# Decay products by doubling on VectorE between projection halves, context units in the down-projection, radix-2 spectra, and a split last projection

## The reference, cut to what matters

```python
def second_block(...):
    h = modulate_2(rmsnorm(x, norm1_g), sh1, sc1)
    hc = modulate_2(rmsnorm(ctx, norm1_g), sh1c, sc1c)
    p, pc = h @ w_in, hc @ w_in                      # 1024 -> 3*512 (Hyena) + 5*512 (HGRN)
    y_hy = hyena_mixer(p[..., :1536], ...)           # y = x2*(h2 * (x1*(h1 * v))), long convolutions by FFT
    y_hg = hgrn_mixer(p[..., 1536:], pc[..., 1536:]) # recurrence, forwards and backwards
    x = x + g1 * (concat(rmsnorm(y_hy), y_hg) @ w_out)
    x = x + g2 * ec_moe(modulate_2(rmsnorm(x, norm2_g), sh2, sc2), router_w, exp_w1, exp_w3, exp_w2)

def gate(z, lb):                                     # per direction
    f = lb + (1 - lb) * sigmoid(z)
    return 1 - f, log(f)                             # key, log of the decay

# S_t = diag(f_t) S_{t-1} + k_t v_t^T ;  o_t = S_t^T q_t ; each scan starts from the context's last state
```

## Time and profile before

| | |
|---|---|
| median of 3 runs | 1800.35 us (1797.34 to 1802.77) |
| profiled execution | 1802.43 us, span 1800.4 us |
| busy PE / DVE / ACT / POOL | 1380.1 / 404.4 / 220.3 / 33.3 us |
| granted TensorE clock over the span | 0.89 |
| bytes moved | 541.98 MB, mean 301 GB/s |

### The profile page before, as it was taken

How to read it: one execution, slowest core, us unless ns; L and a number is a source line. 1 busy time by engine, 2 the same in 40 slices (tenths; PEclk the granted TensorE clock), 3 DMA queues, 4 the chain that set the end, 5 groups by cost and what they waited for, 6 DMA issues and landing times.

```text
span 1800.4 us, 17839 instructions
## 1 busy us (share of the span) xinstructions
PE 1380.1 (77%) x7548; PEld 781.6 (43%) x7548; DVE 404.4 (22%) x787; ACT 220.3 (12%) x383; POOL 33.3 (2%) x63
## 2 busy tenths in 40 slices
PE   6989999999999999898875655665655655665655
PEld 3756678888877777897431111111111111111111
DVE  3635642232023234452320000000000000000001
ACT  2313422121021012221200000000000000000001
POOL 1100000000000010000000000000000000000000
PEclk8989999999999999998998788788788887788787
DMA  9775947565476221003999999999999999999996
GB/s 360 180 190 201 318 146 263 190 210 211 174 270 197 70 74 47 1 1 145 394 415 428 428 429 428 429 428 429 429 428 428 428 429 428 428 429 428 428 428 271
DMA packets 103591, 541.98 MB, mean 301 GB/s; under 512 B 5555, under 2 KB 66644, under 8 KB 72372
## 3 DMA queue, kind: packets, MB, share of 16 engines
q1 hardware_dynamic: 100204, 531.65, 75.0%
q0 software_dynamic: 1328, 6.69, 0.9%
q10 hardware_dynamic: 2008, 2.89, 0.5%
HBM read 537.02 MB, written 4.19 MB: 301 GB/s over the span
## 4 chain that ended last, share of the span: by engine, by line
PE 49%; DMA 44%; DVE 4%; ACT 2%; issue 1%; SPq 0%; DVEq 0%
DMA ring<-in_exp_w_dram 43%; PE L L1485 17%; PE L L1643 4%; PE X L1881 4%; PE L L1496 3%; PE X L1899 3%; PE L L1688 2%; PE L L1761 2%; PE L L1619 2%; DMA ring<-in_w_ada_dram 2%; PE X L1778 1%; PE X L1432 1%; PE X L1670 1%; PE X L1677 1%; PE L L1470 1%; PE L L1432 1%
## 5 line engine op out<-in xcount | busy, mean ns | idle before, releaser
L1485 PE MATMUL L<-tok,ring 128*128 128x256 f32 x1280 | 286.6, 384 | 2.4 <-ACT tok L601 1.6
L1485 PEld LDWEIGHTS L<-tok,ring 128*128 128x128 f32 x1280 | 244.7, 193 | 50.2 <-issue 17.3
L1881 PE MATMUL X<-ring,HR 128*32 128x512 f32 x960 | 164.7, 823 | 123.7 <-DMA ring<-in_exp_w_dram 123.7
L1899 PE MATMUL X<-ring,HI 128*32 128x512 f32 x1024 | 172.6, 811 | 96.3 <-DMA ring<-in_exp_w_dram 89.3
L1881 PE MATMUL X<-arena,HR 128*32 128x512 f32 x960 | 143.3, 725 | 93.9 <-DMA arena<-in_exp_w_dram 93.5
L1881 PEld LDWEIGHTS X<-ring,HR 128*32 128x32 f32 x960 | 30.8, 131 | 252.7 <-DMA ring<-in_exp_w_dram 195.9
L1899 PEld LDWEIGHTS X<-ring,HI 128*32 128x32 f32 x1024 | 33.3, 131 | 218.0 <-DMA ring<-in_exp_w_dram 143.2
L1312 DVE TENSOR_TENSOR HR<-HR,X 128x512 f32<-128x512 f32 x16 | 11.0, 687 | 511.6 <-ACT HR L816 511.6
L1881 PEld LDWEIGHTS X<-arena,HR 128*32 128x32 f32 x960 | 28.4, 123 | 207.2 <-DMA arena<-in_exp_w_dram 149.8
L816 ACT ACTIVATE HR<-X 128x512 f32<-128x512 f32 x16 | 9.6, 597 | 807.4 <-PE X L1881 807.4
L1643 PE MATMUL L<-arena,ring 128*128 128x256 f32 x352 | 76.8, 380 | 0.0
(11 more groups left out here) (338 smaller groups left out, 1234.8 us busy)
## 6 DMA issues: line engine op xcount, KB each, us to landing
ring<-in_exp_w_dram SPq DMA_DIRECT2D x128, 2048.0 KB, 25.9
arena<-in_exp_w_dram SPq DMA_DIRECT2D x63, 2048.0 KB, 26.2
ring<-in_w_in_dram SPq DMA_DIRECT2D x28, 1024.0 KB, 12.2
ring<-in_w_ada_dram SPq DMA_DIRECT2D x24, 1024.0 KB, 7.6
ring<-in_ada_w_dram SPq DMA_DIRECT2D x24, 1024.0 KB, 5.0
ring<-in_w_up_dram SPq DMA_DIRECT2D x22, 1024.0 KB, 5.6
ring<-in_w_down_dram SPq DMA_DIRECT2D x11, 1024.0 KB, 5.0
ring<-in_w_out_dram SPq DMA_DIRECT2D x8, 1024.0 KB, 5.5
```

The source lines that it names most:

```text
L1485: last = MM(L[:, j % 4, m * T:m * T + T], w[:, k, m * P:m * P + P], src(k), start=(k == 0), stop=(k == KT - 1))
L1881: last = MM(X[CAP * j:CAP * j + CAP, w, :], tokens_, mslot(e, u)[:, j * 512:j * 512 + 512], start=(k == 0), stop=(k == KT - 1))
L1899: last = MM(X[CAP * g:CAP * g + CAP, 2, :], hTe[:, 2 * x + c, CAP * j:CAP * j + CAP], mslot(e, u)[:, c * D + nb * 512:c * D + nb * 512 + 5 ...
```

## The change

Four things are done.

1. **Spectra.** The forward and inverse passes of the long convolutions, and of the filters, work on even and odd positions apart (`parity`), with 128x128 tables. A pass is four 512-wide matmuls in place of eight; sums and differences of the halves are formed on DVE (`filter_halves`, `spectra`), and ACT copies the odd parts.
2. **Context.** The six units of the context are loaded a second time as `cin` and multiplied after down-projection units 0 to 3, 5 and 6. ACT forms gates and keys (`forget`'s twin for the context), and DVE multiplies keys by decay products with `climb` and `merge`: a block of length m takes the product of the neighbouring block, and products are merged to blocks of length 2m. PE turns the keys after `wdn` 8 and forms the states after `wdn` 9.
3. **Recurrence.** Logarithms, exponents, exponentials and 0/1 matrices go. Per level DVE multiplies half the queries of each direction (`climb`) and four quarters of the keys by decay products (`level`), POOL copies the two middle quarters between buffers, and one `gram` per level serves both directions at once, nine in all. The grams stand between half units (`half`) of the projection. The order of the units in `win2` is changed for that. The lower bounds of the gates are worked out in the first block as columns (16 small numbers per partition).
4. **Last projection.** `wout2_part` multiplies the Hyena half of all four units first and the other half later. A unit is done with its second half. There are 123 units now, and `wout2` (119 to 122) stands in slots 7, 0, 1, 2.

The core of the diff:

```diff
-WIN2 = (0, 1, 2, 3, 4, 5, 6, 7, 14, 15, 8, 9, 10, 11, 12, 13)
+WIN2 = (0, 1, 2, 3, 6, 7, 10, 11, 12, 13, 4, 5, 14, 15, 8, 9)
+HY_U, Q_U, F_U, G_U, I_U = (0, 1, 2, 3, 4, 5), (6, 7), (10, 11, 12, 13), (14, 15), (8, 9)
+CTX_U = F_U + I_U
+GRAM_BANK = (2, 2, 2, 0, 2, 0, 2, 0, 2)
+CTX_FILL = {0: 0, 1: 1, 2: 2, 3: 3, 5: 4, 6: 5}
...
         u += [("wdn", i)] + [("ada2", m) for m in WDN_FILL.get(i, ())]
+        u += [("cin", CTX_U[CTX_FILL[i]])] if i in CTX_FILL else []
...
+            for n in range(1, NL + 1):
+                pool.wait_ge(S["tree_ready"], n)
+                nc.gpsimd.tensor_copy(quarters(uA[n % 2], LEVELS[n - 1])[:, :, 1:3, :], quarters(uB, LEVELS[n - 1])[:, :, 1:3, :]
+                                      ).then_inc(S["middle_copied"], 1)
...
+            def forget(i):
+                d = i // 2
+                forgotten(unit_out("f", i), fT, d, i % 2, "lin_emptied_by_act", emptied[pos["f"][i]][1])
+                for h in (2 * (i % 2), 2 * (i % 2) + 1):
+                    for x in range(2):
+                        kept(parity((uA[0] if x == d else uB)[:, h, :], x), parity(fT[:, d, h, :], x), HG * d + h)
+                        last = decayed(parity(fT[:, d, h, :], x), HG * d + h)
+                last.then_inc(S["lat_gates"], 1)
...
+            def filter_halves(o):
+                for i, h in ((0, HR), (2, HI)):
+                    bank = L[:, pos["HF"][4 * o + i] % 4, :]
+                    out_of_bank(dve, "HF", 4 * o + i + 1)
+                    dve.wait_ge(S["HF_done"], 4 * o + i + 1)
+                    V.tensor_tensor(h[:, o, 0, :], bank, h[:, o, 1, :], ALU.add)
+                    e_, o_ = (bank, h[:, o, 1, :]) if i == 0 else (h[:, o, 1, :], bank)
+                    done(V.tensor_tensor(h[:, o, 1, :], e_, o_, ALU.subtract), "lin_emptied_by_dve")
...
+                for v, d, x in ((q, 1, 1), (q, 0, 0), (k, 0, 0), (k, 1, 1)):
+                    if v is not None:
+                        last = V.tensor_tensor(half(v, d, x), half(v, d, x), product(1 - d if v is q else d, 1 - x), ALU.mult)
+                return last
+
+            def merge(m, f):
+
+                g = blocks(f.rearrange("p d h t -> p (d h t)"), m)
+                link(V.tensor_tensor(g[:, :, 0, 0], g[:, :, 0, 0], g[:, :, 1, 0], ALU.mult))
+
+            dve.wait_ge(S["ctx_gates"], 4)
+            for m in LEVELS + (P,):
+                last = climb(m, fC, uC)
+                if m < P:
+                    link(last)
+                    merge(m, fC)
+            done(last, "ctx_keys")
             residual("wdn", lambda k: mod1[:, 40 + k:41 + k])
...
+            def level(n):
+
+                m = LEVELS[n - 1]
+                dve.wait_ge(S["gram_done"], n + 1)
+                climb(m, fT, None, vT)
+                now, then, other = quarters(uA[(n - 1) % 2], m), quarters(uA[n % 2], m), quarters(uB, m)
+                fwd, bwd = quarters(fT[:, 0, :, :], m), quarters(fT[:, 1, :, :], m)
+                for to, x, by, y in ((then, 0, fwd, 1), (then, 3, bwd, 2), (other, 1, bwd, 0), (other, 2, fwd, 3)):
+                    if x == 1:
+                        dve.wait_ge(S["middle_copied"], n)
+                    last = V.tensor_tensor(to[:, :, x, :], now[:, :, x, :], by[:, :, y, 0:1].broadcast_to([P, HG * T // (4 * m), m]), ALU.mult)
+                done(last, "tree_ready")
+                dve.wait_ge(S["tree_ready"], n + 1)
+                merge(m, fT)
...
-                    for t in range(TT):
-                        last = MM(bank, dftE[:, i // 2, t, (i % 2) * P:(i % 2) * P + P], hsd[:, o, t, i // 2, :], start=(t == 0), stop=(t == TT - 1))
-                    last.then_inc(S["HF_done"], 1)
...
+                    MM(aux("HF", 4 * o + i), dftE[:, i // 2, i % 2, :], hsd[:, o, i % 2, i // 2, :], start=True, stop=True).then_inc(S["HF_done"], 1)
...
             def forward_dft(o, src):
                 for part in range(2):
-                    for f in range(2):
-                        for t in range(TT):
-                            last = MM(X[:, 2 * part + f, :], dft[:, part, t, f * P:f * P + P], src(t), start=(t == 0), stop=(t == TT - 1))
+                    for x in range(2):
+                        last = MM(X[:, 2 * part + x, :], dft[:, part, x, :], src(x), start=True, stop=True)
                 last.then_inc(S["dft_done"], 1)
...
+            half("hy", 4, 0)
+            gram(0)
+            half("hy", 4, 1)
+            gram(1)
+            half("hy", 5, 0)
+            hyena_turn(4)
+            half("hy", 5, 1)
+            gram(2)
+            hyena_turn(5)
+            for x, (name, i) in enumerate((("g", 0), ("g", 1), ("i", 0))):
+                half(name, i, 0)
+                gram(3 + 2 * x)
+                half(name, i, 1)
+                gram(4 + 2 * x)
+            unit("i", 1)
...
+            for i in range(4):
+                wout2_part(i, range(HG))
+                if i == 2:
+                    reached(pe, "o_normed")
...
             for i in range(4):
-                features("wout2", i, pos["wout2"][i], lambda k: yTh[:, k, :] if k < HG else yTg[:, k - HG, :])
+                wout2_part(i, range(HG, KT))
```

More of the change, by code:

```diff
@@ new lines, in _ @@
+            taps(0)
+            taps(1)
+            natural(0)
+            taps(2)
+            natural(1)
+            odd_parts(0)
+            taps(3)
+            natural(2)
+            silu("q", qT, 0)
+            silu("q", qT, 1)
+            natural(3)
+            forget(0)
+            odd_parts(1)
+            for i in range(1, 4):
+                forget(i)
+            taps(4)
+            natural(4)
+            taps(5)
+            natural(5)
+            for i in range(2):
+                silu("g", gateT, i)
@@ new lines, in spectra @@
+                dve.wait_ge(S["odd_copied"], o + 1)
+                for part in range(2):
+                    even, odd = X[:, 2 * part, :], U[:, part, 1, :]
+                    V.tensor_tensor(U[:, part, 0, :], even, odd, ALU.add)
+                    last = V.tensor_tensor(odd, even, odd, ALU.subtract)
+                link(last)
+                UR, UI = flat(U[:, 0, :, :]), flat(U[:, 1, :, :])
+                V.tensor_tensor(flat(y1[:, :, :]), UR, hi, ALU.mult)
+                V.tensor_tensor(flat(y2[:, :, :]), UI, hr, ALU.mult)
@@ L1155, in _ @@
+            done(V.tensor_tensor(flat(vT[:, 1, :, :]), flat(qT), flat(fT[:, 0, :, :]), ALU.mult), "tree_ready")
+            gather(0)
+            dve.wait_ge(S["tree_ready"], 1)
+            level(1)
             short_conv(4)
+            gather(1)
             short_conv(5)
-            gated(0, znat, "z_ready")
-            out_of_bank(dve, "win2", 7)
-            V.tensor_scalar(qT[:, :, :], qT[:, :, :], P ** -0.5, None, ALU.mult)
-            spectra(1)
+            level(2)
             gated(1, y1, "y_nat")
+            gather(2)
@@ L1162, in _ @@
+            for n in range(3, NL + 1):
+                level(n)
+                gather(n)
+            dve.wait_ge(S["gram_done"], NG)
+            done(climb(P, fT, None, vT), "tree_ready")
             dve.wait_ge(S["y_nat"], 1)
@@ L1704, in _ @@
-            unit(8)
+            unit("f", 0)
             pe.wait_ge(S["z_ready"], 1)
             forward_dft(1, lambda t: znat[:, t, :])
-            unit(9)
-            pe.wait_ge(S["ctx_ready"], 8)
-            both(10)
+            for i in range(1, 4):
+                unit("f", i)
             inverse_dft(1)
-            both(11)
-            reached(pe, "y_normed")
-            for c in range(HG):
-                for t in range(TT):
-                    last = nc.tensor.transpose(X[:, 2 + c // 2, (c % 2) * T + t * P:(c % 2) * T + t * P + P], y1[:, t, c * P:c * P + P], ident)
@@ L1728, in sq @@
-            def sq(i):
-                return sqc[:, i, :]
-            pe.wait_ge(S["sqc_landed"], 16)
-            pe.wait_ge(S["log_ready"], 2)
-            for b, terms in enumerate((((SQ_SX, 0), (None, 1)), ((SQ_SX, 1),), ((SQ_PX, 0),), ((None, 0), (SQ_PX, 1)))):
-                for n, (mat, t) in enumerate(terms):
-                    last = MM(X[:, b, :], ones if mat is None else sq(mat), gc[:, b // 2, t, :], start=(n == 0), stop=(n == len(terms) - 1))
-            last.then_inc(S["ctx_decay_done"], 1)
```

587 lines of the change are left out of this document (285 added, 302 removed).

## The result

The changed kernel takes 1714.55 us (median of four runs, 1712.43 to 1715.83); beside it the kernel before took 1800.82. The ratio is 0.9523, with a 95% interval from 0.951 to 0.9535: 86.3 us less. The profiled execution took 1712.43 us with a span of 1710.0, against 1800.4 before. Run once more beside other kernels, it took 1712.82 (four runs, 1712.41 to 1713.5; ratio 0.9512). Predicted were 1710 us, and 1700 to 1730 as the range.

The account below looks back on a forecast made before the run. The bound was taken as the instant the expert stream gets going, set by the second output projection, plus a fixed stream. Projection -94.8 and stream +4.7 gave -90.1 us, so 1800.35 became 1710 us, range 1700 to 1730.

Parts of the forecast that it names:

- Part 1, -5.0: Filter spectra (104 to 147 us): halved passes -6.9, waiting +0.8, gate-bound operations +1.1, sum -5.0 us.
- I allow 0.4 of waiting per filter: Filter spectra: PE waits 0.4 us per filter for VectorE's halves, +0.8 us in all.
- The piece of 1.1: Filter stage: six small gate-bound operations join the VectorE chain PE waits for until 103 us, +1.1 us.
- Part 2: Context in the down-projection: PE gets 46.9 us more there, VectorE's 14.3 us climb is hidden, tokens ready at 563.8.
- Part 3, 189.4: Tokens to output projection's end: PE work 180.4 plus waits 9.0 us, ending at 753.2 instead of 847.96.
- turns 4 and 5 behind their short convolutions, which stand behind a level, 2.4 and 1.0: Among the 9.0 us of exposed waits before the projection's end: PE waits 2.4 and 1.0 us at these turns.
- a rival of 0.08 with +5 to +8: PE's clock falls in the new gaps of 1 to 2.4 us; if twice, +5 to +8: 1716; chance 0.08.
- the rival of scattered operands: Grams 1 and 2 and their quarter products cost double for jumping operands: +7, 1717 us; chance 0.05.
- The rival of 1724 to 1730: VectorE sets the tree's pace: narrow forms cost half as much again, 7.5 us a level against 5.24; chance 0.13.
- Some 0.8 us: GpSimd's copy of the middle quarters, 512 elements, in each level, with 4.0 us of cover.
- Part 4, +4.7: Expert stream: 3.4 MB less loaded ahead costs 7.9 us, 3.2 us comes back, net +4.7.
- The refund: Expert stream: its near standstill with all buffers full (157 GB/s at 875), a 3.2 us loss, will not recur.

## Why the prediction was right, and where it was off

**What bounds it.** Right: the end is the end of the output projection plus a fixed stream. E is 952.4 before and 949.8 to 952.9 in every kernel here but the one with nothing loaded ahead, while the projection's end lay anywhere from 728.98 to 847.96.

**Part 1, -5.0.** Measured: the first block's output projection ends 4.8 us sooner. This is right by two errors that cancel. "I allow 0.4 of waiting per filter" holds for the first (0.35) and fails for the second (3.25), whose halves stand behind VectorE's reciprocal; 2.7 of it the moved halves gave back. Against it the stage began 1.5 sooner in this profile instead of 1.1 later. That is luck: the projection unit near 40 us took 7.14 us instead of 9.25, at a granted clock of 1.00 instead of 0.81, and the one ahead of the filter 8.56 instead of 9.15, at 0.81 instead of 0.76. The piece of 1.1 itself was right. From the end of the first of these units to the start of the second 56.5 us pass, and 55.5 before: 1.0.

**Part 2.** Right: tokens at 564.41 against 563.8, and the context's cost reaches the end (30 us by ratio for 31.1 of work cut). The climb took 14.8 us for 14.3 and is hidden.

**Part 3, 189.4.** It took 194.35. Up to gram 0 it is exact (91.38 against 91.4). Between gram 0 and gram 3, where its terms add up to 24.4, it is 3.9 over. The step that was off is the wait list's "turns 4 and 5 behind their short convolutions, which stand behind a level, 2.4 and 1.0": 3.3 and 1.0, and then 0.6 + 0.9 us of slower PE, which I had held apart as a rival of 0.08 with +5 to +8. The convolution's move took these 4.8 us away together; they are 2.4 over their term. Gram 1 is 0.85 over, the small core of the rival of scattered operands (it said +7). Grams 0, 2 and 3 take some 2.0 us instead of 1.79, in all 0.7, and 1.0 is left in small pieces. The read-out's normalisation is hidden, as forecast, and exposing it cost 7.3 us.

**VectorE's tree.** The forecast that it balances PE holds: behind gram 3 no gram waits, and they are 5.24 us apart. Behind gram 3 climb and quarters take 2.7 us a level for the 3.0 taken. Level 2's merge of 512 elements at 1.10 and the quarters of level 1 at 0.54 are dearer than taken, by 0.4 for the one merge and 0.5 for the four quarters, and both lie ahead of gram 3. The rival of 1724 to 1730 did not come about. What keeping the half units between the grams is worth I would have underestimated by more than half.

**GpSimd.** "Some 0.8 us" holds for the copy alone, and all seven stayed below the 4.0 us of cover. But the time of six of them is set by VectorE. The seven copies have 512 elements each; in the first they lie in runs of two, in the last in runs of 128. The first, second and sixth of them, with the merge (L1186) that began just ahead of each but the first:

```profile
655.80 0.65 POOL L520 COPY arena<-arena 128x512 f32<-128x512 f32 x1 [222.94 <-DVE tok L1289]
...
667.51 1.23 DVE L1186 TENSOR_TENSOR arena<-arena 128x1024 f32<-128x1024 f32 x1
667.54 1.70 POOL L520 COPY arena<-arena 128x512 f32<-128x512 f32 x1 [11.09 <-DVE arena L1270]
...
699.28 0.27 DVE L1186 TENSOR_TENSOR arena<-arena 128x64 f32<-128x64 f32 x1
699.31 0.72 POOL L520 COPY arena<-arena 128x512 f32<-128x512 f32 x1 [4.41 <-DVE arena L1270]
```

The first copy, the most scattered of all, has no merge beside it and takes 0.65 us. Each of the other six begins 0.02 to 0.03 us behind a merge and ends 0.47 to 0.50 us behind the merge's end, whether the merge lasts 1.23 us or 0.22. So the copy makes no headway while the merge runs, and the length of its runs does not count. The Trainium skill (SBUF — State Buffer, "SBUF: two separate sides") has the two engines lock each other out for the whole instruction, and the trace agrees, with the roles the other way round than in the prediction: the merge comes first and GpSimd waits. The merges pay nothing, as they last as long as those of the context with GpSimd at rest (1.23 and 1.10 us). No VectorE product with two inputs from SBUF began during a copy here, so what one would pay isn't shown.

**Part 4, +4.7.** This was mis-sized. "3.4 MB less is 7.9 us" is right as bytes: 2.8 MB ahead against 6.3, and losing the last 2.9 costs their time one for one. The refund is wrong: not 3.2 us from one dip, but all that the stream of before lost against 428 GB/s in 92 us, 2.9 MB or 6.7 us, which by the bytes leaves about 1.4. The last weights land 936.9 us after the projection's end, against 936.2: +0.8 in place of +4.7. The tail behind the last landing was 14.3 us after and 16.2 before. It is 14.2 to 14.3 or 15.6 to 16.2 in all profiles here, with the same code, and edited kernels show either. So I don't count it as an effect of the change, though the kernel before has one profile only.

**The sum.** Projection -89.2, stream +0.8, tail -2.0: -90.4 in the spans, as measured; forecast -90.1. That the sum fits this closely is luck. The projection's end was missed by 5.6 (0.6 ahead of the tokens, 5.0 in part 3), part 4 was put 3.9 too high, and the tail gave 2.0 that the sum did not have. The prediction then took the difference of the spans for that of the medians. The profiled run of the kernel before lay 1.6 above its median and this one's 2.1 below its own, hence 86.3 between the medians and 1714.55 instead of 1710.

## What to carry to other kernels

Where PE has independent work, put it between the steps of a chain that alternates with VectorE: it hides the chain, and PE does not come back from the wait at a lower clock, which here made the same grams 1.6 to 2.1 times as long. When a step is placed inside a longer one, list what stands behind it on the same engine and who waits there: both costly waits of this change were VectorE's order, and a few moved lines took them. Count a head start in full only up to the point at which the buffers are full, and read what the stream lost afterwards over its whole beginning, not in the one dip that catches the eye.

## What the runs showed of the hardware

- **Strides.** A two-input VectorE product of 512 elements takes 0.69 us in the climb and 1.10 in the merge of level 2, whose elements are 16 bytes apart; of 1024 at 8 bytes 1.23, of 256 at 32 bytes 0.63. The Trainium skill (Advanced Engine Details and Errata, "SBUF Cachelines") states a penalty where subsequent accesses fall on different 16-byte lines. The trace agrees for 16 bytes, at 2.1 ns an element against 1.2 to 1.35, and shows none at 8. The quarters of level 1, single elements 16 bytes apart, take 0.54 us per 256 elements, also 2.1 ns each; those of level 2, in runs of two, 0.34.
- **Moving operand.** A gram whose moving operand changes place after each element took 2.65 us, against 1.80 with the operand in one contiguous run, both at a granted clock of 1.00. With a change after every two elements it was 2.13 against 1.95.
- **GpSimd.** A copy of 512 elements takes 0.65 us alone, in runs of two elements. Behind a VectorE product with two inputs from SBUF that began 0.03 us sooner it takes 1.70, 1.55, 1.08, 0.83, 0.72 and 0.67 us as that product shrinks from 1.23 to 0.22 us, and always ends 0.47 to 0.50 us behind it.
- **Clock.** After 3.3 us of waiting PE's next half unit took 4.34 to 5.91 us for 3.46. After waits of 1.0 us or less none was longer than 3.47. With 2.7 us of waiting in each 5.9 to 6.5, the granted clock was 0.59 over 48 us. One and the same projection unit near 40 us took 7.14 to 10.11 us from profile to profile.
